# One expert's down product moved inside the next expert's gate and up product, with the gate and up weights as two transfers of 2 MB

## The chip, the cores and the metric

The kernel runs on one core of a Trainium2 chip. A time is the device time of one execution in microseconds, and the number to compare is the median of the runs. One more execution was taken with the hardware profiler. All views and rows here come from it.

## What is computed

One step of a decoder layer for 512 prompt tokens and 8 sample tokens (520 in all), model width 1024, in float32. Four mixers run side by side and are projected back. After them comes a mixture of experts with 32 experts of width 512, in which every token goes to two experts. The change touches the experts alone. Per expert the reference computes this:

```python
def run(args):
    xi, e = args
    a, b = jnp.split(xi @ w_gu[e], 2, axis=-1)
    return (jax.nn.silu(a) * b) @ w_down[e]
```

`w_gu[e]` is 1024 x 1024 float32, 4 MB. `w_down[e]` is 512 x 1024, 2 MB. The result rows are scaled by the gates and added to the tokens' rows.

## The kernel before

The first 375 us of the program are the mixers, the output projection and the routing. Then comes the stage of the experts. With these inputs it is one round over the 32 experts, each with a capacity of 64 slots for each half of the model width (all 128 partitions are used, as two halves of 64).

Weights. There are three homes for the weights of an expert, `gu_w[g]` and `down_w[g]`, and expert e uses home e % 3. SyncE (SP) issues all weight transfers on one queue, in the order of the experts. `load_gu` (L574 to L582) cuts the 4 MB into `GU_PARTS` (4) transfers of 1 MB, two of the eight chunks of 128 input channels each, and `load_down` (L584 to L589) issues two transfers of 1 MB. From expert 3 on each transfer waits until the product three experts earlier has read that part: `gu_part_done[part]` or `down_half_done[half]`. The first three experts are loaded during the output projection.

TensorE. `expert` (L1504 to L1531) does one expert after the other: eight chunks c of the gate and up product, each started when its part has landed (`gu_loaded`), then `turn_tokens` for the next expert (four transposes of gathered rows), then the transposes of this expert's hidden rows (`hid_made` to `xt_turned`), then the down product in two halves after VectorE's copy `hT`. Two small tables, `gate_table` and `slot_table`, are made on TensorE ahead of expert 0 and expert 31. `mm` is L1099, `turn` is L1102.

ScalarE. For each expert the SiLU (L1082) and then the scaled copy of the down product out of PSUM (L1086), which raises `y_copied`.

VectorE. For each expert the product with the up half (L2067), the copy of the next expert's tokens `copy_xe` (L2063), the copy `hT` (L2071).

GpSimd. Three indirect DMAs for each expert, in this order: the two scatters with addition of the result rows (L757, `add_rows`), which wait for `y_copied` and for both scatters of the expert before, and then the gather of the tokens of the third expert on (L752).

In the trace the homes are named reg_a, reg_b and reg_w for the gate and up weights and reg_a, reg_b and reg_h for the down weights.

Of the kernel before, what the change touches and what calls it, by code (L numbers as in the profile page):

```python
# [40 lines left out]
N_EXP = 32  # L41
DE = 512
CAP = 64
GU_PARTS = 4
ROUNDS = -(-T // CAP)
EPS = 1e-6
NEG = -1e30
# [132 lines left out]
def layer_kernel(nc, a, o):  # L180
# [7 lines left out]
    with ctx:  # L188
# [115 lines left out]
        hT = [reg_y.cut(256, "p (c s) -> p c s", c=2) for _ in range(2)]  # L304
# [180 lines left out]
        def _(sp_eng):  # L485
# [124 lines left out]
            eng.wait_ge(bank_full[bank_of["NT3"]], turn_of["NT3"] + 1)  # L610
            load_down(2, 2)
            eng.wait_ge(bank_full[bank_of["Y3.0"]], turn_of["Y3.0"] + 1)
            load_gu(2, 2, parts=(0, 1))
            eng.wait_ge(bank_full[bank_of["Y3.1"]], turn_of["Y3.1"] + 1)
            load_gu(2, 2, parts=(2, 3))
            load_experts(0)

            eng.wait_ge(S["rounds_made"], 1)
# [164 lines left out]
        def _(eng):  # L783
# [292 lines left out]
            rounds = eng.value_load(n_rounds[0:1, 0:1], min_val=1, max_val=ROUNDS)  # L1076
            eng.sem_inc(S["y_copied"], 2)

            def expert(e, n, b, reused=None):

                eng.wait_ge(S["gu_done"], n + 1)
                eng.activation(silu[b], bank[2 + b][:, 0:256], ACT.Silu, scale=slot_scale[:, 1, bass.ds(e, 1)]).then_inc(S["silu_done"], 1)  # L1082
                eng.wait_ge(S["down_done"], n + 1)
                if reused is not None:
                    eng.wait_ge(y_scattered[b], reused)
                eng.activation(y_out[b], bank[6 + b][:, :], ACT.Copy, scale=slot_scale[:, 0, bass.ds(e, 1)]).then_inc(S["y_copied"], 1)  # L1086

            with eng.Fori(0, rounds) as r:
                eng.wait_ge(S["round_open"], r + 1)
                eng.wait_ge(S["slot_gates_made"], r + 1)  # L1090
                for b in range(2):
                    expert(b, N_EXP * r + b, b)
                with eng.Fori(1, N_EXP // 2) as i:
                    for b in range(2):
                        expert(2 * i + b, N_EXP * r + 2 * i + b, b, 16 * N_EXP * r + 32 * i)
        @block.tensor
        def _(eng):
            def mm(out, lhsT, rhs, start, stop):
# [402 lines left out]
            eng.wait_ge(S["rounds_made"], 1)  # L1501
            rounds = eng.value_load(n_rounds[0:1, 0:1], min_val=1, max_val=ROUNDS)

            def expert(n, b, g, loads, gathered):  # L1504


                eng.wait_ge(S["xe_made"], n + 1)
                for c in range(KC):
                    part, within = divmod(c, KC // GU_PARTS)
                    if within == 0:  # L1510
                        eng.wait_ge(gu_loaded[g][part], loads)
                    for s in range(2):
                        w = gu_w[g][:, c, :].rearrange("p (h f) -> p h f", h=2)[:, :, 256 * s:256 * s + 256]
# [12 lines left out]
                for s_in in range(2):  # L1526
                    eng.wait_ge(down_loaded[g][s_in], loads)
                    for k in range(2):
                        for s in range(2):
                            ins = mm(bank[6 + b][64 * s:64 * s + 64, :], hT[b][:, k, 64 * s_in:64 * s_in + 64], down_w[g][:, s_in, k, 512 * s:512 * s + 512], s_in == 0 and k == 0, s_in == 1 and k == 1)  # L1530
                    ins.then_inc(down_half_done[s_in], 1)  # L1531

            with eng.Fori(0, rounds) as r:
                turn_tokens(0, 256 * r + 16)
                gate_table()
                with eng.Fori(0, N_EXP // 6) as i:
                    for j in range(6):
                        g = j % 3
                        expert(N_EXP * r + 6 * i + j, j % 2, g, 16 * USES[g] * r + 32 * i + 16 * (j // 3) + 16, 256 * r + 48 * i + 16 * ((j + 1) // 2) + 16)
                for e in range(N_EXP - N_EXP % 6, N_EXP):  # L1540
                    g = e % 3
                    if e == N_EXP - 1:
                        slot_table(r + 4)
                    expert(N_EXP * r + e, e % 2, g, 16 * USES[g] * r + 16 * (e // 3) + 16, 256 * r + 16 * ((e + 1) // 2) + 16 if e + 1 < N_EXP else None)


        @block.vector
        def _(eng):
# [239 lines left out]
            h = m[3]  # L1788
# [276 lines left out]
            def expert(n, b, last):  # L2065
                eng.wait_ge(S["silu_done"], n + 1)
                tt(hid[b], silu[b], bank[2 + b][:, 256:512], ALU.mult).then_inc(S["hid_made"], 1)  # L2067
                if not last:
                    copy_xe(n + 1, 1 - b)
                eng.wait_ge(S["xt_turned"], n + 1)  # L2070
                eng.tensor_copy(hT[b], bank[4 + b][:, 0:256].rearrange("p (k s) -> p k s", k=2)).then_inc(S["hT_made"], 1)  # L2071

            with eng.Fori(0, rounds) as r:
                n = N_EXP * r
                copy_xe(n, 0)
                eng.wait_ge(S["gates_tabled"], r + 1)
                eng.tensor_reduce(slot_scale, bank[0][:, 64:256].rearrange("p (x f e) -> p x e f", x=2, f=3), X_AXIS, ALU.add).then_inc(S["slot_gates_made"], 1)
                with eng.Fori(0, N_EXP // 2 - 1) as i:
                    for b in range(2):
                        expert(n + 2 * i + b, b, False)  # L2080
                expert(n + N_EXP - 2, 0, False)
# [4 lines left out]
                expert(n + N_EXP - 1, 1, True)  # L2086
                eng.wait_ge(S["round_scattered"], r + 1)
                eng.tensor_copy(row_of, row_next).then_inc(S["idx_made"], 1)
                eng.sem_inc(S["round_open"], 1)
# [29 lines left out]
```

## Time and profile before

| | us |
|---|---|
| median of 3 runs | 862.53 (862.05 to 862.95) |
| the profiled execution, its own time | 862.31 |
| span of the profile | 860.6 |
| TensorE busy | 733.6 (85%) |
| transfers of queue q1 (SyncE's) | 231.48 MB, 68.2% of 16 DMA engines |

The profile's page gives busy time, the span in 40 slices of 21.5 us, the DMA queues, the chain of work that ended last, the costliest groups of instructions and the DMA issues. Engines are PE (TensorE matmul), PEld (its weight load), DVE (VectorE), ACT (ScalarE), POOL (GpSimd), SP (SyncE). SPq is SyncE's sequencer, which issues DMAs. In a row of instructions "x16" is a count, and "[0.55 <-DMA ...]" is the idle time before the group and what ended it. Of the matmuls of a gate and up product a chunk of 128 channels is four records (x4) and the whole product is x32. The down product is x16.

### The profile page before, as it was taken

The page shows a single profiled execution, that of the slowest core. Times are in us where ns is not written, and L with a number is a line of the kernel's source. Part 1 is how long each engine was busy: PE and PEld are TensorE (multiplying, and loading weights), DVE is VectorE, ACT ScalarE, POOL GpSimd, SP SyncE. Part 2 cuts the span into 40 slices and gives each one's busy share as a digit, 9 for nine tenths or more (in the row PEclk, how much of TensorE's full clock was granted, in tenths as well). Part 3 has the DMA queues.
Part 4 walks back from the last instruction along what each step waited for, and adds up shares of the span by engine and source line. Part 5 has one row for each costly group of instructions (what it writes and reads, how often), then busy time and mean ns, then how long its engine had stood idle before and what let it go on. Part 6 is the DMA issues. An engine that isn't in the chain of part 4 may idle for free.

```text
span 860.6 us, 10187 instructions
## 1 busy us (share of the span) xinstructions
PE 733.6 (85%) x3636; PEld 383.0 (45%) x3636; DVE 205.5 (24%) x570; ACT 146.0 (17%) x352; POOL 188.3 (22%) x188
## 2 busy tenths in 40 slices
PE   3999999999998999769999997777787877777783
PEld 3788778887866545433333332222222222222220
DVE  4241101385869300730111010100100100100120
ACT  4122412106354411101000010000000000000000
POOL 7010000070300100013223323123123122132121
PEclk9999999999998999979999999999999999999998
DMA  9652643120530397459999999999999999999992
GB/s 311 130 154 62 194 143 108 42 75 1 179 117 1 141 424 319 163 197 411 414 406 411 412 406 410 411 415 409 412 417 405 416 413 408 416 416 409 414 417 76
DMA packets 77013, 247.04 MB, mean 287 GB/s; under 512 B 24952, under 2 KB 44303, under 8 KB 52363
## 3 DMA queue, kind: packets, MB, share of 16 engines
q1 hardware_dynamic: 63825, 231.48, 68.2%
q0 software_dynamic: 11776, 8.58, 4.5%
q10 hardware_dynamic: 1378, 6.54, 1.9%
q8 instruction: 19, 0.31, 0.2%
q14 instruction: 15, 0.12, 0.0%
HBM read 240.47 MB, written 24.92 MB: 308 GB/s over the span
## 4 chain that ended last, share of the span: by engine, by line
PE 45%; SPq 29%; DMA 16%; DVE 5%; issue 3%; ACT 1%; POOL 1%; ACTq 0%; POOLq 0%; DVEq 0%
PE bank L1099 41%; SPq L582 20%; SPq L589 9%; DMA reg_a<-in_exp_w_gu 6%; DMA reg_b<-in_exp_w_gu 6%; PE bank L1102 4%; DMA ffn_in<-reg_x 1%; DMA reg_x<-in_x_prompt 1%; DVE reg_a L1853 1%; DVE reg_y L2063 1%; ACT reg_y L1082 1%; DVE small L1813 1%; DVE reg_y L2071 0%; DVE reg_y L1860 0%; POOL small L687 0%
## 5 line engine op out<-in xcount | busy, mean ns | idle before, releaser
L1099 PE MATMUL bank<-reg_w,reg_y 128*64 128x512 f32 (+2 forms) x512 | 137.0, 572 | 16.7 <-DMA reg_w<-in_exp_w_gu 16.7
L1099 PE MATMUL bank<-reg_a,reg_y 128*64 128x512 f32 x528 | 122.8, 601 | 22.3 <-DMA reg_a<-in_exp_w_gu 16.6
L1099 PE MATMUL bank<-reg_b,reg_y 128*64 128x512 f32 x528 | 122.7, 599 | 21.3 <-DMA reg_b<-in_exp_w_gu 15.6
L2067 DVE TENSOR_TENSOR reg_y<-reg_y,bank 128x256 f32<-128x256 f32 x32 | 13.5, 421 | 417.5 <-ACT reg_y L1082 417.5
L1099 PEld LDWEIGHTS bank<-reg_w,reg_y 128*64 128x64 f32 (+2 forms) x512 | 45.3, 144 | 96.3 <-issue 53.5
L1099 PE MATMUL bank<-reg_b,reg_w 128*128 128x260 f32 x384 | 85.3, 383 | 0.0
L1099 PEld LDWEIGHTS bank<-reg_a,reg_y 128*64 128x64 f32 x528 | 34.4, 137 | 102.1 <-issue 49.8
L1099 PEld LDWEIGHTS bank<-reg_b,reg_y 128*64 128x64 f32 x528 | 34.7, 136 | 100.2 <-issue 57.6
L1099 PEld LDWEIGHTS bank<-reg_b,reg_w 128*128 128x128 f32 x384 | 72.7, 190 | 12.1 <-issue 1.1
L687 POOL TENSOR_TENSOR small<-small 128x1 f32<-128x1 f32 (+4 forms) x18 | 20.4, 1136 | 194.5 <-DVE small L1902 69.6
L757 POOL DMA_INDIRECT out_y_p<-reg_y,reg_h x16 | 25.3, 1581 | 166.3 <-ACT reg_y L1086 166.3
L1102 PE MATMUL bank<-small,reg_y 128*128 128x128 f32 (+3 forms) x205 | 42.5, 317 | 21.4 <-DVE reg_y L2067 15.0
L757 POOL DMA_INDIRECT out_y_p<-reg_h x16 | 25.3, 1579 | 161.8 <-issue 161.8
L1099 PE MATMUL bank<-reg_w,reg_b 128*128 128x256 f32 (+2 forms) x320 | 60.5, 382 | 0.0
L1082 ACT ACTIVATE reg_y<-bank,small 128x256 f32<-128x256 f32 x32 | 15.2, 474 | 262.7 <-PE bank L1099 262.7
L1099 PEld LDWEIGHTS bank<-reg_w,reg_b 128*128 128x128 f32 (+1 forms) x320 | 50.8, 170 | 8.3 <-ACT reg_a L786 0.4
L1102 PEld LDWEIGHTS bank<-small,reg_y 128*128 128x128 f32 (+3 forms) x205 | 29.5, 202 | 54.1 <-issue 32.0
L1099 PE MATMUL bank<-reg_h,reg_y 128*64 128x512 f32 x160 | 36.5, 598 | 5.2 <-DVE reg_y L2071 5.2
L752 POOL DMA_INDIRECT reg_y<-ffn_in,reg_h x32 | 35.1, 1097 | 21.0 <-issue 18.8
L757 POOL DMA_INDIRECT out_y_s<-reg_y,reg_h x16 | 24.9, 1554 | 4.9 <-issue 4.9
L757 POOL DMA_INDIRECT out_y_s<-reg_h x16 | 24.8, 1553 | 4.9 <-issue 4.9
L1086 ACT ACTIVATE reg_y<-bank,small 128x512 f32<-128x512 f32 x16 | 11.0, 688 | 87.2 <-PE bank L1099 87.2
(343 smaller groups left out, 641.6 us busy)
## 6 DMA issues: line engine op xcount, KB each, us to landing
reg_a<-in_exp_w_gu SPq DMA_DIRECT2D x44, 1024.0 KB, 28.0
reg_b<-in_exp_w_gu SPq DMA_DIRECT2D x44, 1024.0 KB, 27.8
reg_w<-in_exp_w_gu SPq DMA_DIRECT2D x40, 1024.0 KB, 28.1
reg_a<-in_exp_w_down SPq DMA_DIRECT2D x22, 1024.0 KB, 28.1
reg_b<-in_exp_w_down SPq DMA_DIRECT2D x22, 1024.0 KB, 28.3
reg_h<-in_exp_w_down SPq DMA_DIRECT2D x20, 1024.0 KB, 28.0
reg_w<-in_w_in SPq DMA_DIRECT2D x9, 1024.0 KB, 10.7
reg_w<-in_w_out SPq DMA_DIRECT2D x2, 2048.0 KB, 11.2
```

The source lines that it names most:

```text
L582: eng.dma_start(gu_w[g][:, lo:lo + width, :], src).then_inc(gu_loaded[g][part], 16)
L589: eng.dma_start(down_w[g][:, half], src).then_inc(down_loaded[g][half], 16)
L687: eng.tensor_tensor(out, in_, minus_half[0:out.shape[0], 0:out.shape[-1]], ALU.pow).then_inc(S[s_done], 1)
L752: eng.indirect_dma_start(xe_rows[e % 2], None, x1_dram, idx, bounds_check=2 * T - 1, oob_is_err=False).then_inc(x_gathered[e % 2], 16)
L757: eng.indirect_dma_start(y, idx, y_out[e % 2], None, bounds_check=last, oob_is_err=False, compute_op=ALU.add).then_inc(y_scattered[e % 2], 16)
L1082: eng.activation(silu[b], bank[2 + b][:, 0:256], ACT.Silu, scale=slot_scale[:, 1, bass.ds(e, 1)]).then_inc(S["silu_done"], 1)
L1086: eng.activation(y_out[b], bank[6 + b][:, :], ACT.Copy, scale=slot_scale[:, 0, bass.ds(e, 1)]).then_inc(S["y_copied"], 1)
L1099: return eng.matmul(out, lhsT, rhs, start=start, stop=stop, skip_group_check=True)
L1102: return eng.transpose(out, in_, ident[0:in_.shape[0], 0:in_.shape[0]])
L1813: eng.tensor_reduce(att_mx[:, col:col + 1], ps[:, 0:width], X_AXIS, ALU.max, negate=True).then_inc(S["att_max"], 1)
L1853: eng.reciprocal(rs, rs).then_inc(S["nrm_made"], 1)
L2067: tt(hid[b], silu[b], bank[2 + b][:, 256:512], ALU.mult).then_inc(S["hid_made"], 1)
```

## The change

The 4 MB of gate and up weights become two transfers of 2 MB (`GU_PARTS = 2`), and so two semaphores and two signals that a part is free. On TensorE the transposes of expert e's hidden rows and its down product are issued inside the gate and up product of expert e + 1, ahead of chunk 2 and of chunk 4. `turn_tokens` goes ahead of chunk 6, and `gate_table` ahead of chunk 4 of expert 0. The last expert's transposes and down product follow its own gate and up product. ScalarE and VectorE take their steps in the matching order.

```diff
-GU_PARTS = 4
+GU_PARTS = 2
...
-            load_gu(2, 2, parts=(0, 1))
+            load_gu(2, 2, parts=(0,))
...
-            load_gu(2, 2, parts=(2, 3))
+            load_gu(2, 2, parts=(1,))
...
-            def expert(e, n, b, reused=None):
-
+            def gated(e, n, b):
                 eng.wait_ge(S["gu_done"], n + 1)
                 eng.activation(silu[b], ...)
+
+            def rows_out(e, n, b, reused=None):
                 eng.wait_ge(S["down_done"], n + 1)
...
+                gated(0, n, 0)
+                for e in range(2):
+                    rows_out(e, n + e, e)
+                    gated(e + 1, n + e + 1, 1 - e)
+                with eng.Fori(1, N_EXP // 2 - 1) as i:
                     for b in range(2):
-                        expert(2 * i + b, N_EXP * r + 2 * i + b, b, 16 * N_EXP * r + 32 * i)
+                        rows_out(2 * i + b, n + 2 * i + b, b, 16 * N_EXP * r + 32 * i)
+                        gated(2 * i + b + 1, n + 2 * i + b + 1, 1 - b)
...
-            def expert(n, b, g, loads, gathered):
-
+            def gate_up(n, b, g, loads, gathered, between):
 
                 eng.wait_ge(S["xe_made"], n + 1)
                 for c in range(KC):
+                    if c in between:
+                        step, args = between[c]
+                        step(*args)
+                    if c == 6 and gathered is not None:
+                        turn_tokens(1 - b, gathered)
                     part, within = divmod(c, KC // GU_PARTS)
                     if within == 0:
                         eng.wait_ge(gu_loaded[g][part], loads)
...
-                if gathered is not None:
-                    turn_tokens(1 - b, gathered)
+            def turn_hidden(n, b):
                 eng.wait_ge(S["hid_made"], n + 1)
...
                 ins.then_inc(S["xt_turned"], 1)
+
+            def down(n, b, g, loads):
                 eng.wait_ge(S["hT_made"], n + 1)
...
+                def expert(e, i=0):
+
+                    n = N_EXP * r + 6 * i + e
+                    gate_up(n, e % 2, *homes(e, i), tokens_of(e + 1, i), {2: (turn_hidden, (n - 1, 1 - e % 2)), 4: (down, (n - 1, 1 - e % 2, (e - 1) % 3, loads_of(e - 1, i)))})
+
                 turn_tokens(0, 256 * r + 16)
-                gate_table()
...
+                gate_up(N_EXP * r, 0, *homes(0), tokens_of(1), {4: (gate_table, ())})
+                with eng.Fori(0, 5) as i:
+                    for e in range(1, 7):
+                        expert(e, i)
+                for e in range(31, N_EXP):
                     if e == N_EXP - 1:
                         slot_table(r + 4)
+                    expert(e)
+                turn_hidden(N_EXP * r + N_EXP - 1, 1)
+                down(N_EXP * r + N_EXP - 1, 1, (N_EXP - 1) % 3, loads_of(N_EXP - 1))
...
             def expert(n, b, last):
+                hidden_turned(n - 1, 1 - b)
                 if not last:
                     copy_xe(n + 1, 1 - b)
-                eng.wait_ge(S["xt_turned"], n + 1)
-                eng.tensor_copy(hT[b], ...).then_inc(S["hT_made"], 1)
+                gated(n, b)
```

## Rows read from the trace of the kernel before

**Rows 1.** Slices of 21.5 us on the page: granted clock in tenths, GB/s.
```profile
PEclk9999999999998999979999999999999999999998
GB/s 311 130 154 62 194 143 108 42 75 1 179 117 1 141 424 319 163 197 411 414 406 411 412 406 410 411 415 409 412 417 405 416 413 408 416 416 409 414 417 76
```
**Rows 2.** Stretches: length, busy us of PE, PEld, DVE, ACT, POOL; clock, DMA share, GB/s.
```profile
228.00:237.00 9.00, 9.00 (x77) 6.94 (x75) 6.10 (x22) 5.84 (x26) 0.56 (x1) 1.00 1.04 392
297.00:333.00 36.00, 36.00 (x112) 16.58 (x110) 3.65 (x6) 5.21 (x14) 0.56 (x1) 1.00 1.01 423
378.00:385.00 7.00, 6.13 (x32) 2.34 (x28) 1.44 (x3) 0.47 (x1) 0.00 (x0) 1.00 0.93 315
385.00:450.00 65.00, 60.25 (x282) 21.73 (x278) 7.22 (x15) 5.81 (x10) 21.16 (x15) 1.00 1.02 410
450.00:840.00 390.00, 317.54 (x1392) 100.56 (x1386) 38.96 (x85) 29.73 (x51) 107.42 (x76) 1.00 1.02 412
```
**Rows 3.** DMA issues and packets: KB each, median us from issue to landing.
```profile
reg_a<-in_exp_w_gu SPq DMA_DIRECT2D x44, 1024.0 KB, 28.0
DMA packets 77013, 247.04 MB, mean 287 GB/s; under 512 B 24952, under 2 KB 44303, under 8 KB 52363
out_win_s<-in_state_win_kv ACTq DMA_DIRECT2D x1, 2040.0 KB
```
**Rows 4.** TensorE's waits over the whole span: us in total, times, longest.
```profile
PE bank L1099 <- DMA reg_w<-in_exp_w_gu: 16.7, 27, 1.0
```
**Rows 5.** TensorE in order of time, one expert while it does not wait for weights.
```profile
409.63 3.65 PE L1099 MATMUL bank<-reg_h,reg_y 128*64 128x512 f32 x16 [0.52 <-DVE reg_y L2071]
413.11 7.04 PE L1099 MATMUL bank<-reg_a,reg_y 128*64 128x512 f32 x32
420.08 0.75 PE L1102 MATMUL bank<-small,reg_y 128*128 128x128 f32 x4
421.28 0.50 PE L1102 MATMUL bank<-small,reg_y 128*128 128x128 f32 x2 [0.45 <-DVE reg_y L2067]
422.30 3.65 PE L1099 MATMUL bank<-reg_a,reg_y 128*64 128x512 f32 x16 [0.52 <-DVE reg_y L2071]
```
**Rows 6.** All engines in order of time, the start of expert 0.
```profile
373.54 0.69 DVE L2063 TENSOR_TENSOR reg_y<-bank,small 128x512 f32<-128x512 f32 x1 [1.11 <-PE bank L1102]
...
375.03 5.14 PE L1099 MATMUL bank<-reg_a,reg_y 128*64 128x512 f32 x22
...
377.36 2.05 SPq L582 DMA_DIRECT2D reg_a<-in_exp_w_gu  x2
```
**Rows 7.** TensorE in order of time, the last two experts.
```profile
820.00 1.94 PE L1099 MATMUL bank<-reg_a,reg_y 128*64 128x512 f32 x8 [0.55 <-DMA reg_a<-in_exp_w_gu]
...
835.51 1.94 PE L1099 MATMUL bank<-reg_b,reg_y 128*64 128x512 f32 x8 [0.34 <-DMA reg_b<-in_exp_w_gu]
...
840.66 1.94 PE L1099 MATMUL bank<-reg_b,reg_y 128*64 128x512 f32 x8 [0.74 <-DMA reg_b<-in_exp_w_gu]
...
844.82 3.65 PE L1099 MATMUL bank<-reg_b,reg_y 128*64 128x512 f32 x16 [0.52 <-DVE reg_y L2071]
```
**Rows 8.** Granted clock around two idle stretches of TensorE, and their lengths.
```profile
261.57 1.08 PE L1102 MATMUL bank<-small,reg_b 128*128 128x128 f32 x6 [3.05 <-ACT reg_b L965]
264.00:269.00 5.00, 5.00 (x21) 3.38 (x21) 5.00 (x8) 1.83 (x5) 0.00 (x0) 0.50 0.00 0
...
285.00:288.00 3.00, 0.96 (x11) 0.53 (x12) 1.09 (x4) 2.29 (x9) 0.57 (x1) 1.00 0.00 0
```
**Rows 9.** GpSimd's indirect DMAs of one expert, and time to landing (out_y_p, then out_y_s).
```profile
563.86 1.58 POOL L757 DMA_INDIRECT out_y_p<-reg_h  x1 [10.92 <-issue]
565.74 1.55 POOL L757 DMA_INDIRECT out_y_s<-reg_h  x1 [0.30 <-issue]
DMA to landing us min/median/max: 3.7/8.5/9.0
DMA to landing us min/median/max: 2.7/9.1/9.6
```

More of the change, by code:

```diff
@@ L1088, in _ @@
             with eng.Fori(0, rounds) as r:
+                n = N_EXP * r
                 eng.wait_ge(S["round_open"], r + 1)
                 eng.wait_ge(S["slot_gates_made"], r + 1)
-                for b in range(2):
-                    expert(b, N_EXP * r + b, b)
-                with eng.Fori(1, N_EXP // 2) as i:
-                    for b in range(2):
-                        expert(2 * i + b, N_EXP * r + 2 * i + b, b, 16 * N_EXP * r + 32 * i)
+                gated(0, n, 0)
[3 more added lines that the diff above has]
+                with eng.Fori(1, N_EXP // 2 - 1) as i:
+                    for b in range(2):
+                        rows_out(2 * i + b, n + 2 * i + b, b, 16 * N_EXP * r + 32 * i)
+                        gated(2 * i + b + 1, n + 2 * i + b + 1, 1 - b)
+                rows_out(N_EXP - 2, n + N_EXP - 2, 0, 16 * N_EXP * r + 16 * (N_EXP - 2))
+                gated(N_EXP - 1, n + N_EXP - 1, 1)
+                rows_out(N_EXP - 1, n + N_EXP - 1, 1, 16 * N_EXP * r + 16 * (N_EXP - 2))
         @block.tensor
@@ L1512, in expert @@
                     for s in range(2):
-                        w = gu_w[g][:, c, :].rearrange("p (h f) -> p h f", h=2)[:, :, 256 * s:256 * s + 256]
+                        w = (gu_w[g][:, c]).rearrange("p (h f) -> p h f", h=2)[:, :, 256 * s:256 * s + 256]
                         ins = mm(bank[2 + b][64 * s:64 * s + 64, :].rearrange("p (h f) -> p h f", h=2), xe[b][:, c % 4, c // 4, :], w, c == 0, c == KC - 1)
@@ L1533, in _, with loads_of, homes, tokens_of @@
             with eng.Fori(0, rounds) as r:
-                turn_tokens(0, 256 * r + 16)
-                gate_table()
[L1536 to L1541, printed above, removed]
+                def loads_of(e, i=0):
+                    return 16 * USES[e % 3] * r + 16 * (e // 3) + 32 * i + 16
+                def homes(e, i=0):
+                    return e % 3, loads_of(e, i)
+                def tokens_of(e, i=0):
+                    return 256 * r + 16 * (e // 2) + 48 * i + 16 if e < N_EXP else None
+                def expert(e, i=0):
+                    n = N_EXP * r + 6 * i + e
+                    gate_up(n, e % 2, *homes(e, i), tokens_of(e + 1, i), {2: (turn_hidden, (n - 1, 1 - e % 2)), 4: (down, (n - 1, 1 - e % 2, (e - 1) % 3, loads_of(e - 1, i)))})
+                turn_tokens(0, 256 * r + 16)
+                gate_up(N_EXP * r, 0, *homes(0), tokens_of(1), {4: (gate_table, ())})
[3 more added lines that the diff above has]
+                for e in range(31, N_EXP):
                     if e == N_EXP - 1:
                         slot_table(r + 4)
-                    expert(N_EXP * r + e, e % 2, g, 16 * USES[g] * r + 16 * (e // 3) + 16, 256 * r + 16 * ((e + 1) // 2) + 16 if e + 1 < N_EXP else None)
+                    expert(e)
+                turn_hidden(N_EXP * r + N_EXP - 1, 1)
+                down(N_EXP * r + N_EXP - 1, 1, (N_EXP - 1) % 3, loads_of(N_EXP - 1))
         @block.vector
@@ L2063, in copy_xe, with gated, hidden_turned, expert @@
                 tt(xe[b], bank[1][:, :].rearrange("p (c s n) -> p c s n", c=4, s=2), gain_x.rearrange("p s c -> p c s").unsqueeze(3).to_broadcast([128, 4, 2, CAP]), ALU.mult).then_inc(S["xe_made"], 1)
-            def expert(n, b, last):
+            def gated(n, b):
                 eng.wait_ge(S["silu_done"], n + 1)
                 tt(hid[b], silu[b], bank[2 + b][:, 256:512], ALU.mult).then_inc(S["hid_made"], 1)
+            def hidden_turned(n, b):
+                eng.wait_ge(S["xt_turned"], n + 1)
+                eng.tensor_copy(hT[b], bank[4 + b][:, 0:256].rearrange("p (k s) -> p k s", k=2)).then_inc(S["hT_made"], 1)
+            def expert(n, b, last):
+                hidden_turned(n - 1, 1 - b)
                 if not last:
                     copy_xe(n + 1, 1 - b)
-                eng.wait_ge(S["xt_turned"], n + 1)
-                eng.tensor_copy(hT[b], bank[4 + b][:, 0:256].rearrange("p (k s) -> p k s", k=2)).then_inc(S["hT_made"], 1)
+                gated(n, b)
             with eng.Fori(0, rounds) as r:
@@ L2077, in _ @@
                 eng.tensor_reduce(slot_scale, bank[0][:, 64:256].rearrange("p (x f e) -> p x e f", x=2, f=3), X_AXIS, ALU.add).then_inc(S["slot_gates_made"], 1)
+                copy_xe(n + 1, 1)
+                gated(n, 0)
                 with eng.Fori(0, N_EXP // 2 - 1) as i:
                     for b in range(2):
-                        expert(n + 2 * i + b, b, False)
-                expert(n + N_EXP - 2, 0, False)
+                        expert(n + 2 * i + b + 1, 1 - b, False)
                 ts(pk_next, pk_next, float(-CAP), None, ALU.add).then_inc(S["next_at"], 1)
@@ L2086, in _ @@
                 expert(n + N_EXP - 1, 1, True)
+                hidden_turned(n + N_EXP - 1, 1)
                 eng.wait_ge(S["round_scattered"], r + 1)
```

## The prediction

> **What bounds the kernel now.** I read the slices of the page first. From the slice at 387 us to that at 839 us the DMA engines move 405 to 417 GB/s [rows 1], whatever TensorE does. The stretches say the same more finely: 410 GB/s from 385 to 450 us, 412 GB/s from 450 to 840 us, at a DMA share of 1.02 [rows 2]. In the second stretch TensorE is busy 317.5 of 390 us. Then I read TensorE's waits: in the experts it waits for gate and up weights (16.7 us in 27 waits for one of the three homes, and the other two are alike) [rows 4], and per expert 0.45 us for the gated product and 0.52 us for VectorE's copy of the turned hidden rows [rows 5]. The last two, 31 us over 32 experts, are what the change covers with other matmuls. A weight transfer lands 28.0 us after its issue [rows 3]: eleven transfers of 1 MB are queued at any time, so the queue never runs dry while TensorE is a few us late. So the stage of the experts ends when about 29 experts' weights (182 MB) have gone through a saturated queue, plus what TensorE still has to do after the last landing. What the 31 us of waits cost is nothing, except where they lie outside the stream: at its start and at its end. I therefore cost three things: when the stream starts, how fast it runs, and what follows it.
>
> **The start of the stream.** The first freed part lets SP issue at 377.36, after two chunks of expert 0, which starts at 375.03 [rows 6]. After the change the first free part is four chunks. A chunk is a quarter of the 3.48 us that 16 matmuls take from start to start (409.63 to 413.11 [rows 5]), 0.87 us, so two more chunks are +1.74 us. Against it, `gate_table` no longer stands ahead of expert 0: this then starts when the token copy is done, 373.54 + 0.69 = 374.23 and a little, say 374.35, 0.68 us earlier. The clock is at half there until about 375.5 (the fall and the return of the clock can be seen in the slice before [rows 1]), and 0.68 us at half clock does 0.34 us of work: 1.74 - 0.34 = +1.4 us. TensorE now idles between the transposes and expert 0, so the clock may come back later. A half clock during all of the four chunks would add about 1.7 us more. Second, the first down transfer. Now `down` of expert 0 waits inside expert 1: 3.48 + 0.9 (gate table at full clock, half of its length in the trace) + 3.48 + 0.7 (token transposes) of expert 0, then 3.48 of four chunks, 0.4 of the hidden transposes and 1.74 of the first down half. That is 14.2 us after 374.35 plus 0.56 for the half clock, 389.1, and the issue then takes effect 1 to 2 us later (between 377.36 and the full rate of 385 us the queue moved 315 GB/s over 7 us [rows 2], a loss of about 1.6 us). The 4 MB ahead of it last from the issue at 378.8 for 10.2 us at 411 GB/s plus that 1.6 us, to 390.6. The hole is 0 to 1 us; I take 0.5. From expert 1 on the frees run ahead: TensorE takes 12.67 us an expert (409.63 to 422.30 [rows 5]) or less, the queue 15.7. Start: I take +2.5 us, with ends of +1.4 and +5.
>
> **The rate of the stream.** Each piece of 8 KB of a partition's row becomes one of 16 KB. In the trace 24,650 packets have 8 KB or more [rows 3], and the experts' 192 transfers of 128 rows make 24,576, so a contiguous run is one packet. The 74 others have to hold one copy of 2040 KB [rows 3], so packets over 8 KB exist. What a packet costs beside its bytes: output weights came as 2 KB packets at 392 GB/s, experts' weights with no other traffic as 8 KB packets at 423 GB/s [rows 2]. Per engine (a sixteenth) that is 83.6 ns and 309.9 ns, so 6 KiB more cost 226.3 ns. That is 37.7 ns per KiB (27.15 GB/s, 434 GB/s for 16 engines), 75.4 ns for 2 KiB, and 8.2 ns of each packet are left as fixed. An expert's gate and up weights are 32 packets per engine now, 16 after: 16 x 8.2 = 0.13 us an expert, 3.8 us over 29. Ends: nothing, if packets or their cost stay as they are, and -7.5 us, if the gate and up weights ran at the 434 GB/s of no fixed cost at all (2.6% of the 9.9 us that 4 MB last, 29 times). I take -3.8.
>
> The two sizes of transfer: at 28 us of queue [rows 3] a transfer's own latency is hidden, and 1 MB transfers reach 423 GB/s. So I give the 2 MB as such nothing. The Trainium skill ("DMA: Bandwidth & Descriptors", the section on measured bandwidth) has 341 GB/s for one transfer of 1 MB and 425 for one of 16 MB and advises large ones. That is a single transfer with its latency in the sum, and this case's 423 GB/s with 1 MB speaks against taking it over here. By it the change would gain several per cent of the stream.
>
> **The end.** Expert 31's last weights before the two down halves landed at 840.66, its second quarter at 835.51 [rows 7]. These are the landings of its two 2 MB parts after the change. Before, three of the four quarters were done when the last landed, and the down product began at 844.82. After, TensorE does from 835.51: four chunks 3.48, hidden transposes of expert 30 0.4 (0.50 less overlap [rows 5]), the whole down product of expert 30 3.48, and only then the last four chunks, 3.65 to their end: 846.5 instead of 840.66 + 1.94 = 842.6. SiLU, gating, transposes, copy and down of expert 31 follow as before, uncovered. That is +3.9 us. The down product of expert 30 had stood in time in which TensorE otherwise waits for expert 31. It now waits for half of expert 31's weights. `slot_table` of the last expert is no later than 835.5: expert 30 ends at 820.00 + 11.65 = 831.65, and SiLU, gating and the slot comparison last 3 us.
>
> The clock belongs here. TensorE's work per expert after the change is 6.97 + 0.7 + 0.5 + 3.48 = 11.65 us [rows 5], and a period is 15.7 us (835.51 less 820.00 is 15.5 [rows 7]). The idle time, so far three or four pieces of 0.5 us for weights and three more, becomes one of some 4 us. After an idle stretch of 3.05 us the granted clock was 0.50 for over 5 us, while around one of 2.04 us (0.96 of 3 us busy) it stayed at 1.00 [rows 8]. So I expect the clock to fall once per expert. In the middle this costs nothing: a half clock for 6 us adds 3 us to 11.65, still under 15.7, and a longer one would close the idle time that causes it. At the end it is uncovered: 0 to 3.4 us, and I take 1.5. End: +5.4 us, with ends of +3.9 and +7.3.
>
> **Edits with one answer.** ScalarE's copy ahead of the next SiLU: the down product ends 4.3 us before the gate and up product that the SiLU waits for, and the copy is 0.7. VectorE's new order is that of TensorE's signals. The hidden rows' copy has four chunks' halves (1.74 us) as cover and needs 0.4 us and a signal. None is on the path.
>
> **Sum.** +2.5 - 3.8 + 5.4 = +4.1 us on the profiled execution's own 862.31 (its span of 860.6 and 1.7 around it), 866.4. The median of the runs is 0.22 above it: 866.6.
>
> **The rivals.**
> A. The packets stay at 8 KB, or their cost is in the bytes: no gain in the stream. For: the only copy with larger packets is not from HBM to SBUF. Start and end alone: 862.5 + 7.9 = 870.4.
> B. The stream gains enough to pay for both ends. For: the line through the two rates leaves 423 GB/s still 2.6% under its limit of 434, and the gain is multiplied by 29 experts while the losses come once. Point from which it decides: 0.22 us an expert. With the bound of 7.5 us, +1.4 at the start and +3.9 at the end it gives -2.2: 860.3. Against: the same line puts only half of this bound on the packets that the change removes, the other half on those that stay.
> C. GpSimd's chain becomes the bound. A scatter is issued only after both of the expert before have landed. Its second is issued 1.88 us after the first and lands after 9.1 us in the median, while the shortest, with no weights in flight, took 2.7 [rows 9]. So the loaded weight transfers add about 6 us to each, and the chain's own period is 1.88 + 9.1 + 0.9 = 11.9 us of 15.7. If this 6 us is a count of weight packets that go first, doubled packets double it for the share that is gate and up weights: 9.1 becomes 12 to 15, and the chain 15 to 18 us. It decides from a landing time of 12.9 us. With 0.6 us an expert over the 15.6 of the stream, for 24 experts, it adds 14 us: 880. Against: the landing time did not move with where in a transfer the scatter fell (the first of the two has a median of 8.5 and a maximum of 9.0 over all experts [rows 9], though TensorE's period of 12.67 us up to 450 us moves it against the transfers of 2.6 us). The Trainium skill ("DMA: Bandwidth & Descriptors", "Queues, rings and completion order") says that a DMA engine drains a whole packet of one queue, typically 9 to 17 descriptors, before it turns to another; by that a transfer's share of an engine would be the unit, doubled here. The narrow spread in this trace speaks against so coarse a unit.
>
> **How the numbers follow.** Forecast (all three terms near their values, 863.9 to 869) 0.50; A 0.20 (869 to 873); B 0.18; C 0.12. B splits: 0.08 end more than 0.2% under 862.53, 0.10 within it. About 0.2% (1.7 us) is what a measurement of this kernel can tell from no change. Forecast and B's upper edge touch there, so same gets 0.03 more. Faster 0.08, same 0.13, slower 0.79. The range runs from 862.5, which leaves out the most of B, to 873.5, which leaves out C.
>
> **What would show it.** The DMA share still 1.0 from about 387 to 843 us. The first reissue of weights at 378.8 rather than 377.4, or about 380.5 if the clock stays low. TensorE's waits for VectorE gone but for one expert, and in their place about one wait of 4 us per expert for the first part, with a clock below 1 in the slices. The rate between 450 and 840 us at 415 or more (by A 412). The last down product begins 5 us or so later after the last gate and up landing than the 4.2 us of before. For C: waits of GpSimd gone from `y_copied`, landings of 13 us, a DMA share under 1. The prediction is wrong if the rate rises by over 1.5%, or if TensorE's low clock reaches into the stream.

## The result and the profile after

The changed kernel takes 897.86 us in the median of 4 runs (893.38 to 902.50). The kernel before takes 862.74 (4 runs). The ratio is 1.040 (95% interval 1.037 to 1.042), so the change costs 35 us. The forecast was 866.6 with a range of 862.5 to 873.5: the sign was right, the size far off, and it was rival C, with 12% and 14 us, that came true, at more than twice its price.

The page of the kernel after, slices of 22.5 us: granted clock in tenths, DMA share, GB/s.

```profile
PEclk9999999999979999698898898798899899998898
DMA  9642823010700992499999999999999999999800
GB/s 310 114 145 59 263 111 92 24 48 1 283 1 4 400 397 106 145 363 415 423 383 417 417 398 417 411 398 415 415 419 384 417 419 410 414 380 417 347 6 10
```

Against [rows 1] three things are new. The stream of weights has dips (383, 398, 384, 380), and it ends two slices before the program does: for the last 48 us no weights are loaded. Before, the weights ended some 4 us before TensorE's last product did. And the clock is below 1 in many slices.

Stretches of the kernel after (columns as in [rows 2]).

```profile
297.00:333.00 36.00, 36.00 (x111) 16.43 (x110) 3.65 (x6) 5.20 (x14) 1.10 (x2) 1.00 1.01 426
450.00:840.00 390.00, 313.46 (x1330) 108.55 (x1328) 37.75 (x74) 28.32 (x49) 101.18 (x72) 0.90 1.01 408
850.00:880.00 30.00, 27.26 (x120) 9.27 (x118) 5.30 (x16) 2.32 (x4) 5.68 (x5) 0.88 0.07 12
```

The first row has only weight transfers in it and is where 16 KB packets show their rate: 426 GB/s for 423 before. (Gate and up weights come as 16 KB packets here, down weights as 8 KB ones in every kernel of this document.) From 450 to 840 us the kernel after moves 408 GB/s where it was 412. In the third row TensorE still works off experts whose weights landed long before.

Why does it lag? TensorE's and GpSimd's waits of the kernel after (us in total, times, longest):

```profile
PE bank L1110 <- DMA reg_y<-ffn_in,reg_h: 102.4, 23, 7.4
...
POOL out_y_p L757 <- DMA out_y_s<-reg_y,reg_h: 138.5, 12, 12.9
POOL out_y_p L757 <- DMA out_y_s<-reg_h: 100.5, 9, 12.3
...
SPq L582 <- PE bank L1107: 288.8, 32, 35.8
```

TensorE no longer waits for weights at all (no such row, against [rows 4]). It waits 102 us for gathers of tokens, 23 times. GpSimd now waits for its own scatters in 21 of 31 experts. And SyncE waits 289 us for TensorE to free a gate and up home, where it waited 97 us before. The roles are turned round: the queue of weights waits for the compute, and the compute for GpSimd's small indirect DMAs.

GpSimd in order of time, one expert of the kernel after and the next one's first scatter, and then times from issue to landing between 450 and 840 us (gathers, out_y_s):

```profile
637.01 1.58 POOL L757 DMA_INDIRECT out_y_p<-reg_h  x1 [11.38 <-DMA out_y_s<-reg_y,reg_h]
638.89 1.55 POOL L757 DMA_INDIRECT out_y_s<-reg_h  x1 [0.30 <-issue]
640.75 1.08 POOL L752 DMA_INDIRECT reg_y<-ffn_in,reg_h  x1 [0.30 <-issue]
652.84 1.58 POOL L757 DMA_INDIRECT out_y_p<-reg_y,reg_h  x1 [11.01 <-DMA out_y_s<-reg_h]
...
DMA to landing us min/median/max: 5.7/13.0/15.0
DMA to landing us min/median/max: 7.4/13.1/15.0
```

The median landing of 9.1 us (out_y_s in [rows 9], and gathers the same) is 13.0 and 13.1 us. From scatter to scatter that is 1.88 + 13.1 + 0.9 = 15.9 us, and the two rows show 652.84 - 637.01 = 15.83.

TensorE in order of time in the kernel after, around one of its waits for a gather, and the stretch behind the wait (columns as in [rows 2]):

```profile
840.62 1.89 PE L1107 MATMUL bank<-reg_w,reg_y 128*64 128x512 f32 x8
848.18 1.10 PE L1110 MATMUL bank<-small,reg_y 128*128 128x128 f32 x4 [5.68 <-DMA reg_y<-ffn_in,reg_h]
849.21 3.68 PE L1107 MATMUL bank<-reg_w,reg_y 128*64 128x512 f32 x8
852.68 2.36 PE L1107 MATMUL bank<-reg_a,reg_y 128*64 128x512 f32 x8
854.97 0.51 PE L1110 MATMUL bank<-small,reg_y 128*128 128x128 f32 x2
855.41 1.94 PE L1107 MATMUL bank<-reg_a,reg_y 128*64 128x512 f32 x8
857.18 3.60 PE L1107 MATMUL bank<-reg_h,reg_y 128*64 128x512 f32 x16
...
849.30:852.60 3.30, 3.30 (x8) 0.92 (x10) 0.69 (x1) 0.00 (x0) 2.24 (x2) 0.50 0.39 69
```

Six of eight chunks are done, then TensorE idles 5.68 us for the tokens of the next expert, of which this expert's last two chunks have no need. They stand behind the transposes on the engine. After the idle time the eight matmuls of two chunks last 3.68 us instead of 1.9: the granted clock was 0.50 in this stretch (last row). The down product of this same expert stands inside the next one and begins only 9 us after the wait (857.18). Its rows are what GpSimd needs before it issues its scatters and, behind them, the next gather.

### The profile page after: what moved, and what is told of

It reads as the page before. It is cut to its first block, busy times and chain, and to the rows that moved or that the text cites. A ratio compares the mean times of both kernels' runs of the same rounds, so it can differ in the third digit from the quotient of the medians.

```text
span 898.4 us, 10039 instructions
## 1 busy us (share of the span) xinstructions
PE 751.1 (84%) x3636; PEld 396.3 (44%) x3636; DVE 208.4 (23%) x570; ACT 145.9 (16%) x352; POOL 188.8 (21%) x188
## 4 chain that ended last, share of the span: by engine, by line
PE 49%; DMA 36%; issue 7%; DVE 3%; POOL 3%; ACT 1%; POOLq 0%; SPq 0%; ACTq 0%; DVEq 0%
PE bank L1107 44%; DMA out_y_s<-reg_y,reg_h 12%; DMA reg_y<-ffn_in,reg_h 11%; DMA out_y_s<-reg_h 11%; PE bank L1110 5%; POOL out_y_s L757 1%; DMA ffn_in<-reg_x 1%; POOL out_y_p L757 1%; DMA reg_x<-in_x_prompt 1%; DVE reg_a L1881 1%; ACT reg_y L1087 0%; DVE small L1841 0%; POOL small L687 0%; DVE reg_h L1588 0%; DVE reg_a L1858 0%
## 5 line engine op out<-in xcount | busy, mean ns | idle before, releaser
L1107 PE MATMUL bank<-reg_w,reg_y 128*64 128x512 f32 (+2 forms) x512 | 148.8, 624 | 0.0
L1107 PE MATMUL bank<-reg_a,reg_y 128*64 128x512 f32 x528 | 133.4, 637 | 0.9 <-DVE reg_y L2091 0.9
L1107 PE MATMUL bank<-reg_b,reg_y 128*64 128x512 f32 x528 | 133.3, 636 | 0.5 <-DVE reg_y L2099 0.5
L1110 PE MATMUL bank<-small,reg_y 128*128 128x128 f32 (+3 forms) x205 | 47.1, 348 | 103.5 <-DMA reg_y<-ffn_in,reg_h 102.4
L1110 PEld LDWEIGHTS bank<-small,reg_y 128*128 128x128 f32 (+3 forms) x205 | 31.8, 204 | 156.6 <-issue 134.9
L2091 DVE TENSOR_TENSOR reg_y<-bank,small 128x512 f32<-128x512 f32 x32 | 22.1, 692 | 323.7 <-PE bank L1110 323.7
L1107 PEld LDWEIGHTS bank<-reg_w,reg_y 128*64 128x64 f32 (+2 forms) x512 | 48.5, 156 | 71.5 <-issue 68.8
L1107 PEld LDWEIGHTS bank<-reg_b,reg_w 128*128 128x128 f32 x384 | 72.7, 190 | 12.1 <-issue 1.1
L1107 PEld LDWEIGHTS bank<-reg_a,reg_y 128*64 128x64 f32 x528 | 38.1, 146 | 74.3 <-issue 72.2
L1107 PEld LDWEIGHTS bank<-reg_b,reg_y 128*64 128x64 f32 x528 | 38.2, 146 | 73.8 <-issue 71.0
L1087 ACT ACTIVATE reg_h<-bank,small 128x512 f32<-128x512 f32 x16 | 11.0, 687 | 111.0 <-PE bank L1107 111.0
## 6 DMA issues: line engine op xcount, KB each, us to landing
reg_w<-in_w_in SPq DMA_DIRECT2D x9, 1024.0 KB, 10.8
```

Of the source, the lines that this page charges most:

```text
L1107: return eng.matmul(out, lhsT, rhs, start=start, stop=stop, skip_group_check=True)
L1110: return eng.transpose(out, in_, ident[0:in_.shape[0], 0:in_.shape[0]])
```

## The experiments

Theory P, formed from these rows: an indirect DMA waits behind a number of weight packets, so 16 KB packets lengthen each one, and two loops that go through GpSimd then bound the experts' stage. The first goes from scatter to scatter. The second goes from gather over the token transposes, the rest of that expert, the down product inside the next, ScalarE's copy and the two scatters to the gather after next. The rivals are that the new order alone is the cause (O), or that the size of a transfer and not of its packets is (T).

### One part of the change at a time

```diff
 e1_order_only: the kernel after, with
-GU_PARTS = 2
+GU_PARTS = 4
 e2_parts_only: the kernel before, with
-GU_PARTS = 4
+GU_PARTS = 2
```

> The new order of the products, with the gate and up weights still as four transfers of 1 MB (8 KB of a row each). Theory P (a scatter or gather waits behind a count of weight packets, and packets of 16 KB double that wait): scatters and gathers land after about 9 us again as in the kernel before, GpSimd's chain of 11.9 us stays under the stream's 15.7, TensorE waits for weights again, and the time is that of the kernel before plus the later end: 866 to 868. Rival O (the order itself costs the time: the gather is asked for only after a down product that now comes late): TensorE waits for gathers also here, and the time stays over 885.

Measured: 867.54 us (9 runs), ratio 1.0045 (1.0034 to 1.0057). Scatters (out_y_s) land after 9.1 us again:

```profile
DMA to landing us min/median/max: 8.8/9.1/9.5
```

TensorE waits 60 us for weights, and still 8.9 us in eight waits for gathers behind expert 0's, which the stream covers.

> The old order, with the gate and up weights as two transfers of 2 MB. Theory P: scatters land after about 13 us, GpSimd's chain is 1.9 + 13.1 + 0.9 = 15.9 us an expert from the first expert on, and as GpSimd would have to do 32 of them from 390 us on the time is 885 to 897. Rival O: near the kernel before, 860 to 866, with the landings at 9 or at 13 us but no wait of TensorE for gathers.

Measured: 886.01 us (4 runs), ratio 1.027 (1.024 to 1.030). Landings between 500 and 800 us, gathers and then out_y_s, and GpSimd's waits:

```profile
DMA to landing us min/median/max: 12.7/13.2/13.8
DMA to landing us min/median/max: 12.6/13.1/13.5
...
POOL out_y_p L757 <- DMA out_y_s<-reg_h: 157.0, 14, 13.2
POOL out_y_p L757 <- DMA out_y_s<-reg_y,reg_h: 143.1, 13, 11.9
```

Against the 863.50 us of the kernel before on the same chip the order costs 4.0 us and the parts 22.5 us. Together they cost 35. The parts are the larger cause, O alone falls, and 8 us or so come only from both at once. That a gather which lands late costs more in the new order is the reading for these; e7 and e8 below test its parts. GpSimd's first scatters of successive experts are 15.94 us apart in e2 (407.38 to 821.87, 26 steps), as 1.9 + 13.1 + 0.9 says. The time lies in the range expected.

### Packet or transfer

```diff
 e3_2mb_8kb_rows: the kernel after, with
+CHUNKS = [0, 1, 4, 5, 2, 3, 6, 7]
...
-src = gu_dram[...][:, lo // 4, lo % 4:lo % 4 + width, :]
+src = gu_dram[...][:, :, lo:lo + cols, :]      (cols = width // 2)
 e6_1mb_4kb_rows: the same with GU_PARTS = 4 and CHUNKS = [0, 4, 1, 5, 2, 6, 3, 7]
 e4_1mb_16kb_rows: the kernel after, with
+for at in (0, 64):
+    eng.dma_start(gu_w[g][at:at + 64, lo:lo + width, :], src[at:at + 64])...
```

> As the changed kernel, with two transfers of 2 MB, but each takes 8 KB from each half of the channels, so that a packet has 8 KB as before (chunks are used in the order 0, 1, 4, 5, 2, 3, 6, 7). Theory P: landings of about 9 us, 866 to 870. Rival T (a DMA engine first drains the whole share of a transfer, and 2 MB transfers double it): landings of 13 us and 893 to 902, as the changed kernel.

Measured: 875.30 us (4 runs), ratio 1.0125 (1.010 to 1.015). Gathers and out_y_s, between 500 and 800 us:

```profile
DMA to landing us min/median/max: 8.9/9.3/9.9
DMA to landing us min/median/max: 9.1/9.3/9.7
```

Transfers of 2 MB with packets of 8 KB leave the landings at 9.3 us. T falls, and with it the coarse unit of rival C. The time itself lies above theory P's 866 to 870 us and far below T's 893 to 902. Part of that is a side effect of the edit: each part now touches both halves of the old output weights, so expert 2's weights are asked for at 357.25 us instead of 321.64. They then run beside the store of the rows that are to be gathered, which takes 12.5 us instead of 8.9, and expert 0 starts at 377.92 instead of 374.93 us as in e1. That is 3.0 of the 7.8 us between the two. The rest was not followed further.

> The new order with four transfers of 1 MB, each of 4 KB from each half of the channels: gate and up weights in packets of 4 KB, half of the kernel before. Theory P (an indirect DMA waits behind a count of weight packets, some 20 of them): scatters and gathers land after 6 to 7.5 us instead of 9.1. Rival (a floor of some 9 us that only packets over 8 KB raise): 9 us. The rate of the stream should fall by about 2%, and the time is 872 to 880 either way, since the stream is the bound.

Measured: 879.45 us (2 runs), ratio 1.018 (1.015 to 1.021). Gathers and out_y_s, and the stream:

```profile
DMA to landing us min/median/max: 6.1/6.5/7.9
DMA to landing us min/median/max: 6.8/7.1/8.7
...
450.00:840.00 390.00, 316.92 (x1326) 103.03 (x1322) 36.89 (x72) 28.54 (x49) 101.19 (x72) 0.93 1.03 405
```

The time and the landings are as expected by theory P. With 4, 8 and 16 KB packets of gate and up weights a gather issued right behind the two scatters lands after 6.5, 9.1 and 13.2 us (e6, e1, e2), and the stream runs at 405, 412 and 415 GB/s (the last in e9, below). By the prediction's line (8.2 ns and 37.7 ns per KiB) a packet of 4, 8 and 16 KB takes an engine about 160, 310 and 612 ns. If all the packets in front were gate and up weights, the steps of 2.6 and 4.1 us would be those of 13 to 17 packets, an estimate. The first scatter of the three has smaller steps (7.4, 8.5 and 10.8 us), those of 7 to 8 packets. So the count is no fixed one. Small packets buy latency of everything else and pay with rate.

> As the changed kernel, but each part of 2 MB is issued as two transfers of 1 MB over 64 partitions each, with packets of 16 KB. Theory P: landings of 13 us and 893 to 902 as the changed kernel. Rival T: landings of about 9 us and 866 to 870.

Measured: 1250.82 us in the median of three runs (a fourth took 1302.12), ratio 1.449. Both expectations fail, and the run does not tell P from T. A stretch in which only weights move, and the part of it in which only gate and up weights do:

```profile
297.00:333.00 36.00, 36.00 (x111) 16.65 (x111) 3.65 (x6) 5.20 (x14) 0.67 (x2) 1.00 1.01 244
322.00:333.00 11.00, 11.00 (x33) 5.26 (x32) 1.07 (x3) 2.64 (x6) 0.56 (x1) 1.00 1.02 217
```

Transfers over 64 partitions move 217 GB/s where those over 128 move 423. The 244 has the down weights in it, which still go over 128. That the landings grow to 25.4 us (gathers) at this rate is no evidence on either theory.

### Opening GpSimd's loops

```diff
 e7_gather_ahead: the kernel after, with gather(e + 3) ahead of add_rows(e)
-for e in range(N_EXP):
-    if e + 2 < N_EXP:
-        eng.wait_ge(S["xe_turned"], n + e + 1)
+for e in range(-1, N_EXP):
+    if e + 3 < N_EXP:
+        eng.wait_ge(S["xe_turned"], n + e + 2)
...
-        gather(e + 2)
+        gather(e + 3)
 e8_scatter_waits_split: the kernel after, with a semaphore for each of the two tensors
-eng.wait_ge(y_scattered[(e - 1) % 2], 16 * N_EXP * r + 32 * ((e + 1) // 2))   (ahead of both)
+eng.wait_ge(y_scattered[(e - 1) % 2][k], 8 * N_EXP * r + 16 * ((e + 1) // 2)) (ahead of each)
 e9_both_loops_open: both
```

> As the changed kernel, but GpSimd asks for the gather of expert e + 3 ahead of the scatters of expert e, not behind them. Theory: two loops run through GpSimd, one from scatter to scatter (1.9 + 13.1 + 0.9 = 15.9 us an expert) and one from gather over token transposes and the next down product to the next scatters and gather. This edit opens the second alone: TensorE's 102 us of waits for gathers are gone or small, and the time falls from 898 to that of the parts alone, 886. Rival (the gather loop is the whole loss): under 870.

Measured: 880.10 us (4 runs), ratio 1.019 (1.017 to 1.022).

```profile
PE bank L1112 <- DMA reg_y<-ffn_in,reg_h: 85.8, 27, 7.0
```

The time fell by 18 us, 6 us below the parts alone. One statement of the expectation failed: TensorE's waits for gathers are still 85.8 us. GpSimd issues one gather per pass of its scatters' loop, so TensorE is paced by that loop wherever it happens to wait; that it shows up at the gathers was read, not tested.

> As the changed kernel, but the scatter to the prompt's rows waits only for the last scatter to the prompt's rows, and that to the samples' rows only for that to the samples' rows (they are two tensors). This opens the loop from scatter to scatter (then 13.1 + 0.9 = 14.0 us, under 15.7) and leaves the gather's loop. Theory: the gather's loop is about 31.3 us for two experts, 15.7, so the time falls to 875 to 893. Rival (the scatters' loop is the whole loss): 864 to 869.

Measured: 888.04 us (4 runs), ratio 1.027 (1.025 to 1.030). Waits of TensorE and GpSimd, and then one turn of the gather's loop:

```profile
PE bank L1112 <- DMA reg_y<-ffn_in,reg_h: 96.9, 16, 7.3
POOL out_y_p L760 <- DMA out_y_p<-reg_y,reg_h: 78.7, 11, 7.8
POOL out_y_s L760 <- DMA out_y_s<-reg_y,reg_h: 44.0, 14, 3.5
...
560.45 1.09 POOL L752 DMA_INDIRECT reg_y<-ffn_in,reg_h  x1 [0.31 <-issue]
574.55 1.10 PE L1112 MATMUL bank<-small,reg_y 128*128 128x128 f32 x4 [6.39 <-DMA reg_y<-ffn_in,reg_h]
587.91 0.69 ACT L1089 ACTIVATE reg_y<-bank,small 128x512 f32<-128x512 f32 x1 [8.02 <-PE bank L1109]
593.29 1.08 POOL L752 DMA_INDIRECT reg_y<-ffn_in,reg_h  x1 [0.30 <-issue]
```

GpSimd's waits for scatters have fallen from 239 to 123 us but are not gone. First scatters are now 12 and 20 us apart in turn, 15.96 us in the mean. The 123 us do not lie on the loop: they come ahead of every other pass, while the scatters at 589.55 us, ahead of the gather at 593.29, wait for ScalarE's copy. From gather to gather these rows show 14.1 us until TensorE has the tokens, 14.0 until ScalarE has copied the down product and 4.7 on GpSimd, 32.8 us for two experts. The mean over the run is 32.0. The gather's loop is enough by itself to hold the kernel there.

> As the changed kernel with both edits: gather ahead, and split waits. Theory: the stream is the bound again, at 415 GB/s or more, TensorE waits for weights and neither loop is closed, though scatters still land after 13 us: 864 to 869. Rival (low clock or contention also cost time): over 875.

Measured: 869.13 us (5 runs), ratio 1.006 (1.004 to 1.008), at the upper edge of what was expected. TensorE's waits, landings of out_y_s between 500 and 800 us, and the stream:

```profile
PE bank L1111 <- DMA reg_w<-in_exp_w_gu: 27.3, 8, 4.3
PE bank L1111 <- DMA reg_b<-in_exp_w_gu: 20.9, 8, 4.3
PE bank L1111 <- DMA reg_a<-in_exp_w_gu: 19.5, 8, 4.2
PE bank L1114 <- DMA reg_y<-ffn_in,reg_h: 6.5, 1, 6.5
...
DMA to landing us min/median/max: 10.6/11.2/11.9
...
450.00:840.00 390.00, 319.58 (x1344) 104.40 (x1342) 41.37 (x85) 29.05 (x50) 103.24 (x73) 0.93 1.02 415
```

With both loops open 29 of the 35 us are back. TensorE waits for weights, 24 times and up to 4.3 us (2.8 in the mean), about as the prediction had it, for a gather only ahead of expert 0, and the stream runs at 415 GB/s. Each loop held the kernel while the other was open (888 and 880), so both were closed at nearly the same period. One statement of the expectation failed: scatters land after 11.2 us, not 13, with the same packets. So opening the loops shortened the landings too, and what that alone is worth was not tested. Why they are shorter is open.

### The start and the end

Expert 0's first matmuls, in the kernel of the order alone:

```profile
374.93 6.13 PE L1107 MATMUL bank<-reg_a,reg_y 128*64 128x512 f32 x16 [0.87 <-DVE reg_y L2091]
...
386.00:396.00 10.00, 10.00 (x48) 3.45 (x44) 0.84 (x2) 1.16 (x2) 0.45 (x1) 1.00 0.73 274
```

Four chunks that take 3.65 us at full clock take 6.13, and in the hole after the gate and up weights of expert 3 the queue moves 274 GB/s over 10 us: against the 412 of this kernel's stream that is 3.3 us. The profiled execution is the longest of the nine (869.72 us), so these are upper values for e1.

The end of the stream was priced in three more kernels.

```diff
 e12_last_pair_undone: e9, with
+turn_hidden(N_EXP * r + N_EXP - 2, 0)
+down(N_EXP * r + N_EXP - 2, 0, ...)
+gate_up(N_EXP * r + N_EXP - 1, 1, ..., None, {4: (slot_table, (r + 4,))})
 e10_old_order_2mb_open: the kernel before, with GU_PARTS = 2 and both edits of e9
 e11_last_expert_1mb: e10, with expert 31's weights as four transfers
+    if e == N_EXP - 1:
+        for q in range(4):
+            eng.dma_start(gu_w[e % 3][:, 2 * q:2 * q + 2, :], src).then_inc(last_loaded[q], 16)
```

> As the kernel with the changed order and both loops open (869.1), but the down product of expert 30 stands ahead of expert 31's gate and up product instead of inside it, and the slot table inside. It prices the end of the stream in the new order. Theory: the last down product follows the last gate and up landing sooner by 3 us and the half clock there is gone: 865 to 866.5. Rival (the end costs nothing, the start all): 869.

Measured: 866.85 us (8 runs), ratio 1.0044 (1.003 to 1.006), for e9's 869.13, ratio 1.0061 (1.004 to 1.008). The medians are 2.3 us apart, 1.9 us when each is taken against the kernel before on its own chip, and the intervals overlap. So less came back than the 3 us expected, and it is not clear of the noise.

> The old order of the products with transfers of 2 MB and both loops of GpSimd open (gather ahead, split scatter waits). Theory: the stream bounds; its rate gains 3.8 us, the first free part costs 1.7 us, the last part of 2 MB 1.7 us. Together within 1 us of the kernel before. Rival (2 MB parts lose in another place too): over 866.

Measured: 864.83 us (12 runs), ratio 1.0014 (1.0003 to 1.0025): 1.6 us over the kernel before where at most 1 was expected. Its gathers and then its out_y_s, between 500 and 800 us, and its last down product:

```profile
DMA to landing us min/median/max: 7.9/8.1/10.4
DMA to landing us min/median/max: 10.4/13.1/14.0
...
846.64 5.35 PE L1103 MATMUL bank<-reg_b,reg_y 128*64 128x512 f32 x16 [0.52 <-DVE reg_y L2075]
```

Scatters land after 13.1 us, as in the parts alone, and it costs this kernel next to nothing. The gather is issued some 6 us ahead of the scatters here and lands after 8.1 us, with the same 16 KB packets that gave 13.2. The landing time thus goes also by what GpSimd issued just before, not by the packets alone.

> As the run before it, but the last expert's gate and up weights come in four transfers of 1 MB, so that three quarters of its product are done when the last lands. Theory: 1.7 us less than that run, 1 to 3 us under the kernel before (860 to 862.5). Rival (the last landing does not set the end there): the same time as that run.

Measured: 861.14 us (10 runs), ratio 0.9976 (0.9965 to 0.9986): 2.1 us under the 863.22 of the kernel before on the same chip. It is the one version that beats both kernels. Its last product:

```profile
832.49 5.37 PE L1110 MATMUL bank<-reg_b,reg_y 128*64 128x512 f32 x24
838.23 1.94 PE L1110 MATMUL bank<-reg_b,reg_y 128*64 128x512 f32 x8 [0.37 <-DMA reg_b<-in_exp_w_gu]
```

When the last quarter lands at 838.2 us, three quarters are done. Before, TensorE took it up at 840.66 [rows 7], 2.4 us later: the gain of the larger packets, less the later start. The fall from e10 is 3.7 us where 1.7 were expected. In e10's trace the last down product takes 5.35 us where it takes 3.65 here, at a granted clock of 0.50 from 848 to 850 us. These 1.7 us can be most of the rest. That it is so in every execution of e10 was not shown.

## Why the prediction was wrong, point by point

**What bounds.** The reading of the kernel before holds. The waits that the change covers were worth nothing: the order alone costs 4.0 us and gains none.

**The rate of the stream.** Right. The fixed 8 ns of a packet gave 0.8% for 16 KB packets. The runs have 424 to 426 for 423 GB/s with nothing beside, and 415 for 412 in the stage (e9, e10, e11). In the changed kernel it could not show, since the stream had stopped to be the bound. (Rival B's point of 0.22 us an expert does not follow from the terms beside it: 2.5 + 5.4 over 29 experts is 0.27.)

**The start.** Direction right, size too small. The first reissue came at 381.30 us (profile after) for 377.36 [rows 6], later than even the 380.5 that the text had for a low clock: expert 0 began at 375.80, not 374.35, as its tokens came later, and its four chunks took 5.3 us for 3.5, at a granted clock of 0.58 from 375 to 380 us. The hole at the first down transfer was 3.3 us (e1) for 0.5 assumed. SyncE issued that transfer at 392.32 us in e1, for 389.1 in the sum, and most of the difference is the half clock in the first four chunks (6.1 us for the 4.0 counted). In e1 the start is therefore 1.4 us of reissue and 3.3 us of hole.

**The end.** Right in kind and in size: an idle stretch ahead of expert 31, half clock behind it and expert 30's down product in the way. Expert 31's first matmuls behind the landing and its down product, in e9:

```profile
834.97 3.41 PE L1111 MATMUL bank<-reg_b,reg_y 128*64 128x512 f32 x8 [0.64 <-DMA reg_b<-in_exp_w_gu]
...
849.61 3.65 PE L1111 MATMUL bank<-reg_b,reg_y 128*64 128x512 f32 x16 [0.52 <-DVE reg_y L2103]
```

These are 14.6 us apart, and in the kernel before 844.82 - 835.51 = 9.3 us [rows 7]: +5.3 for the 5.4 put down. Taking the pair apart gave back little of it (e12), since there expert 31's first matmuls stand behind the moved down product and begin only at 838.98.

**The sum.** With GpSimd's loops open the three terms can be seen. The last down product of e9 begins 4.8 us later than before (849.61 for 844.82), where the sum has +4.1. Start and rate together are -0.5 us (834.97 for 835.51) where the text had -1.3. The medians say +5.5 us (869.13 less 863.64), with an interval of 3.5 to 7.1. Some of this agreement is luck: expert 0 began at 373.54 us in e9's profiled execution and at 374.93 in e1's, so its start is flattered, and the hole that the text made too small is smaller there than in e1 (337 GB/s for 274 over the same 10 us).

**The step that failed is rival C**: the sum left the landing time of GpSimd's scatters and gathers at 9.1 us and so put their chain at nothing. They land after 13 us, and the kernel takes 31 us more than the forecast of 866.6. It failed in three places. First, its chance. The text took the narrow spread of landings as evidence against the mechanism. It was evidence only against the coarse unit (a transfer's share), which e3 confirms. It said nothing on the size of a packet, and that is what sets the landing where the order of issue is the same (e2, e3, e6): 7 to 8 packets for the first scatter and 13 to 17 for what follows it, as estimated above.

Second, its price. The text compared the chain's 15 to 18 us with the stream's 15.6 and charged the excess on 24 experts. But the stream has a head start: three experts' weights are there before expert 0 begins, and until these homes are used up GpSimd and TensorE run at 12.67 us an expert. Before, GpSimd's first scatters of expert 0 and 31 are at 389.72 and 850.32 us, a mean of 14.9 us. A chain of 15.9 us that holds from expert 0 on falls 1.0 us behind with each expert, not 0.6 us on 24 of them. It decides from a landing time of 14.9 - 2.8 = 12.1 us, and it takes away the whole lead that the homes gave, which is why the last 48 us of the kernel after have no weights to load. It does not lose all of 31 x 1.0 us: in e2 the scatters of expert 28 are 34.8 us late (837.79 for 803.02), but then the stream is done, landings are short, and the last three steps take 8.4, 12.7 and 13.2 us. The last scatter is 21.8 us late (872.15 for 850.32), and the kernel 22.5.

Third, a loop was missed. The text followed the gather's wait only in so far as it looked at a landing of its own and found idle time to hide it. The new order lengthens the way from a gather to the next one: after the token transposes come two chunks of this expert, four of the next and a down product before GpSimd may go on. In e8 a turn of it is 32 us for two experts: 13 to 14 us of landing, 14 of this work on TensorE and ScalarE (two or three of its chunks at half clock) and 4.7 on GpSimd. e8 shows that this loop holds the kernel alone.

The Trainium skill's rule that a DMA engine drains a whole packet of one queue before it turns to another ("DMA: Bandwidth & Descriptors", "Queues, rings and completion order") was read in the prediction as a transfer's share, and this reading is not borne out: with the transfer doubled and packets of 8 KB (e3) the landings stayed at 9.3 us. The rule itself, with its 9 to 17 descriptors, is neither shown nor refuted here. If a descriptor is one contiguous run of a row, the estimate of 13 to 17 lies in it and that of 7 to 8 just under it.

## What to carry to other kernels

Before enlarging the packets of a saturated queue, list every small DMA that shares the engines and is awaited in a loop, and price its landing time with the new packet size, not with the old one. The same 16 KB packets cost 22.5 us with the loops closed (e2) and 1.6 us with them open (e10). A loop's period is to be compared with the mean period of the whole stage, prefetched lead included, not with the stream's steady period. And before moving work that "only fills idle time", follow which other engine waits for its result: here a transpose that waits for a gather stood ahead of matmuls that did not need it, and the down product that GpSimd needed stood behind both.

## What was not expected of the hardware

- A gather issued right behind two scatters, beside a saturated stream of weights, lands after 6.5, 9.1 or 13.2 us when most of the stream is in packets of 4, 8 or 16 KB (e6, e1, e2). With 16 KB and GpSimd's loops open it was 11.3 us (e9), and 8.1 us when it was issued by itself (e10). The shortest scatter, with no weights in flight, took 2.7 us.
- Transfers of 1 MB over 64 partitions moved 217 GB/s where transfers over 128 partitions moved 423.
- In the kernel after, TensorE idled some 6 us (4.3 to 7.4) for a gather in every other expert or so, and the two chunks of matmuls behind took 2.9 to 3.7 us for 1.9 (granted clock 0.50 where it was read, from 849.3 to 852.6 us). Behind waits under 1.5 us they took 1.9.
